# Paged decode attention interleaved with prompt attention, in bursts of decode steps behind whole head tiles

## The reference, cut to what matters

```python
def diff_attend(q, k, v, q_pos, k_pos, lam):
    s = jnp.einsum('bqhmd,bkhmd->bhmqk', q, k) * (DK_A ** -0.5)
    p = jax.nn.softmax(jnp.where(k_pos[None, :] <= q_pos[:, None], s, -jnp.inf), axis=-1)
    w = p[:, :, 0] - lam * p[:, :, 1]
    return jnp.einsum('bhqk,bkhd->bqhd', w, v)
# prompt: 8 query blocks of 128, 4 heads; sample: 4 new tokens, 4 heads,
pk = cache_k[page_table].reshape(DB, P, H_A, 2, DK_A)
pv = cache_v[page_table].reshape(DB, P, H_A, DV_A)
```

## Time and profile before

| | |
|---|---|
| median of 3 runs | 1150.35 us (1147.07 to 1150.73) |
| the profiled execution | 1145.49 us, span of the core 1143.9 us |
| granted TensorE clock over the span | 0.945 of full speed |
| PE busy | 1006.3 us, 88% of the span |
| DVE / ACT / POOL busy | 521.6 / 419.4 / 138.6 us |
| DMA | 142.08 MB, mean 124 GB/s |

### The profile page before, as it was taken

How to read it: one execution, slowest core, us unless ns; L and a number is a source line. 1 busy time by engine, 2 the same in 40 slices (tenths; PEclk the granted TensorE clock), 3 DMA queues, 4 the chain that set the end, 5 groups by cost and what they waited for, 6 DMA issues and landing times.

```text
span 1143.9 us, 19660 instructions
## 1 busy us (share of the span) xinstructions
PE 1006.3 (88%) x7424; PEld 801.5 (70%) x7424; DVE 521.6 (46%) x1212; ACT 419.4 (37%) x886; POOL 138.6 (12%) x290
## 2 busy tenths in 40 slices
PE   4779999999999999986887788577886999899997
PEld 3679989999888888864655555444555888577773
DVE  4523744554653445433433334167886533442222
ACT  4433353433245434342322223256665323321111
POOL 1300010000000000030333333301100000000000
PEclk8989999999999999988988988779999999999999
DMA  5351215111323222138998995492001032212210
GB/s 180 101 148 50 62 55 131 56 56 56 102 74 91 58 73 75 56 140 252 360 316 315 330 327 198 169 386 97 1 1 60 19 111 74 65 64 83 82 67 23
DMA packets 111249, 142.08 MB, mean 124 GB/s; under 512 B 9256, under 2 KB 75433, under 8 KB 111164
## 3 DMA queue, kind: packets, MB, share of 16 engines
q1 hardware_dynamic: 100924, 107.34, 29.2%
q0 software_dynamic: 10240, 33.56, 8.2%
HBM read 125.47 MB, written 15.41 MB: 123 GB/s over the span
## 4 chain that ended last, share of the span: by engine, by line
PE 69%; DVE 10%; DMA 8%; issue 6%; ACT 4%; POOL 2%; SPq 1%; POOLq 0%; ACTq 0%; DVEq 0%
PE ps L1600 59%; PE ps L1603 9%; DMA Vr<-in_cache_v 4%; DVE pp L1475 3%; DVE pp L1488 2%; DMA Kr<-in_cache_k 2%; DMA wst<-in_w_in 1%; DMA xrow<-in_x_prompt 1%; POOL si L648 1%; DVE hrow L1035 1%; DVE wlo L1041 1%; DVE st L1486 1%; PE ps L1595 1%; ACT on L947 1%; DMA out_k_prompt<-ktok 1%
## 5 line engine op out<-in xcount | busy, mean ns | idle before, releaser
L1600 PE MATMUL ps<-hhi,whi 128*128 128x272 f32 (+1 forms) x672 | 228.2, 340 | 7.0 <-DVE wlo L1041 5.9
L1600 PE MATMUL ps<-hhi,wlo 128*128 128x272 f32 (+1 forms) x672 | 219.0, 326 | 0.0
L1600 PE MATMUL ps<-hlo,whi 128*128 128x272 f32 (+1 forms) x672 | 218.3, 325 | 0.0
L1600 PE MATMUL ps<-wh,r 128*128 128x512 f32 (+1 forms) x576 | 163.3, 401 | 4.6 <-DVE wout_lo L1542 4.6
L1600 PEld LDWEIGHTS ps<-hhi,whi 128*128 128x128 f32 x672 | 128.9, 192 | 18.5 <-DVE wlo L1041 6.1
L1600 PEld LDWEIGHTS ps<-hlo,whi 128*128 128x128 f32 x672 | 128.9, 192 | 9.9 <-issue 1.9
L1600 PEld LDWEIGHTS ps<-hhi,wlo 128*128 128x128 f32 x672 | 128.5, 191 | 9.4
L1600 PEld LDWEIGHTS ps<-wh,r 128*128 128x128 f32 (+1 forms) x576 | 103.4, 182 | 34.4 <-issue 4.9
L1041 DVE TENSOR_TENSOR wlo<-wst,whi 128x1024 fp32r<-128x1024 f32 x56 | 68.6, 1225 | 88.0 <-ACT whi L679 88.0
L1401 DVE COPY kTs<-ps 128x512 f32<-128x512 f32 x64 | 44.3, 692 | 101.3 <-PE ps L1603 101.3
L617 POOL DMA_DIRECT2D Vr<-in_cache_v x128 | 69.1, 540 | 155.8 <-PE ps L1600 131.7
(11 more groups left out here) (307 smaller groups left out, 1542.7 us busy)
## 6 DMA issues: line engine op xcount, KB each, us to landing
Kr<-in_cache_k SPq DMA_DIRECT2D x128, 256.0 KB, 5.6
Vr<-in_cache_v POOLq DMA_DIRECT2D x128, 256.0 KB, 5.5
wst<-in_w_in SPq DMA_DIRECT2D x56, 512.0 KB, 3.9
out_y_prompt<-rows SPq DMA_DIRECT2D x16, 512.0 KB, 2.9
xrow<-in_x_prompt SPq DMA_DIRECT2D x8, 512.0 KB, 4.1
wout<-in_w_out SPq DMA_DIRECT2D x1, 4096.0 KB, 14.1
rows<-in_x_prompt SPq DMA_DIRECT2D x8, 512.0 KB, 4.3
wgate<-in_ple_gate_w SPq DMA_DIRECT2D x2, 2048.0 KB, 21.7
```

The costliest lines, as they stand in the source:

```text
L1600: return nc.tensor.matmul(out, lhsT, rhs, start=start, stop=stop)
```

## The change

The decode's stage is gone; its work is cut into 81 steps and put between the pieces of the prompt attention. Step n turns the keys of group n (over all sequences, 64 groups), turns a part of the weights of the sequence before (4 of its 17 turns in each of steps 3 to 6 of 8, the last in step 7), multiplies the values of group n-12, and scores group n-1. `SHARES` and `DECODED` say after which position steps are done: five lie among the 8 key-and-value pieces of the prompt, and 71 behind the last of the four phases of head tiles 0 to 31, in bursts of 1 (i = 0) to 3 or 4 (i = 7); the last five follow in the drain. Decode has banks 0 to 3 and the prompt attention 4 to 7: one pair of banks for keys (0, 1), one bank (2) for the scores, the turned weights and the `place_q` result, one (3) for values; one pair for head scores (4, 5), one bank (6) for turned weights, one (7) for values. `Kr` shrinks from 16 to 8 slots (4 groups), `S` is there twice (`S0`, `S1`). `w_out` is loaded after the last turn of decode weights, and the gate weights after the last head, since they take over those buffers. SP issues the prompt's key and value outputs and the key pages in the order of the positions.

```diff
+LAST_GROUP = NSEQ * GROUPS
+VALUES_LAG = 12
+STEPS_OF_DECODE = LAST_GROUP + VALUES_LAG + 5
+PHASES = 4
+SHARES = CH * [2.0] + [float(4 + u // H) if u < UNITS and phase == PHASES - 1 else 0.0 for u in range(UNITS + 4) for phase in range(PHASES)]
+POSITIONS = len(SHARES)
+DECODED = [min(STEPS_OF_DECODE - 5, round((STEPS_OF_DECODE - 5) * sum(SHARES[:pos + 1]) / sum(SHARES)))
+           + max(0, pos - POSITIONS + 6) for pos in range(POSITIONS)]
+DECODED = [min(n, STEPS_OF_DECODE) for n in DECODED]
+
+
+def stored(group):
+
+    return group + group // GROUPS + 1
+
+
+def comb_step(seq):
+
+    return GROUPS * (seq + 3) + 1 if seq < NSEQ - 1 else LAST_GROUP + VALUES_LAG + 1
+
+
+COMBINED = {comb_step(seq): seq for seq in range(NSEQ)}
...
+            def key_pages(n):
+                if n % 4 == 0:
+                    page[:] = nc.values_load_multi_w_load_instructions(
+                        ptab[0:1, n * GP:n * GP + GROUPS], engines=[mybir.EngineType.SP], min_val=0, max_val=POOL - 1)[1]
+                if n >= 4:
+                    sp.wait_ge(s["k_used"], n - 3)
+                for k in range(GP):
+                    sp.dma_start(Kr[:, GP * (n % 4) + k, :],
+                                 ck[bass.ds(page[GP * (n % 4) + k], 1), :, :].rearrange("o p d -> (o p) d")
+                                 ).then_inc(k_in[n % 4], 16)
...
+            for pos in range(POSITIONS):
+                if pos < CH:
+                    sp.wait_ge(s["kt_stored"], pos + 1)
+                    sp.dma_start(kp[pos * P:(pos + 1) * P, :], ktok[:, pos % 2, :]).then_inc(k_out[pos % 2], 16)
+                    sp.wait_ge(s["vt_stored"], pos + 1)
+                    put("out_v_prompt", vp[pos * P:(pos + 1) * P, :], vtok[:, pos, :])
+                for n in range(DECODED[pos - 1] if pos else 0, DECODED[pos]):
+                    if n + 4 < LAST_GROUP:
+                        key_pages(n + 4)
...
+            def attend(u, phase):
+                if phase == 0 and u >= 6 and u % H == 2:
+                    heads_square(u // H - 1)
+                if phase == 1 and u < UNITS and not two(u):
                     head_exp(u)
-                if 1 <= u <= UNITS:
-                    weights_out(u - 1)
-                if u >= 2 and (u - 2) % H == H - 1:
-                    heads_square((u - 2) // H)
+                if phase == 1 and 1 <= u <= UNITS:
+                    weights_out(u - 1, 0)
+                if phase == 2 and two(u - 1):
+                    weights_out(u - 1, 1)
+                if phase == 3 and two(u):
+                    head_exp(u)
+
+            for pos in range(POSITIONS):
+                if pos < CH:
+                    keys_out(pos)
+                else:
+                    attend(*divmod(pos - CH, PHASES))
+                for n in range(DECODED[pos - 1] if pos else 0, DECODED[pos]):
+                    decode(n)
...
+            def attend(u, phase):
+                if phase == 0 and u < UNITS:
+                    head_rows(u, 0)
+                if phase == 1:
+                    if u >= 6 and u % H == 2:
+                        heads_scale(u // H - 1)
+                    if u >= 7 and u % H == 3:
+                        heads_gate(u // H - 1)
+                    if 1 <= u <= UNITS:
+                        head_weights(u - 1)
+                if phase == 2 and two(u):
+                    head_rows(u, 1)
...
+            def keys(n):
+                pe.wait_ge(k_in[n % 4], 32 * (n // 4 + 1))
+                if n >= 1:
+                    pe.wait_ge(s["kT_act"], n)
+                    pe.wait_ge(s["kT_dve"], n)
+                for h in range(H):
+                    for k in range(GP):
+                        last = turn(ps[:, h // 2, ((h % 2) * GP + k) * P:((h % 2) * GP + k + 1) * P],
+                                    Kr[:, GP * (n % 4) + k, h * P:(h + 1) * P])
+                last.then_inc(s["k_used"], 1)
+            def scores(m):
+                i, g = divmod(m, GROUPS)
+                pe.wait_ge(s["kT_act"], m + 1)
+                pe.wait_ge(s["kT_dve"], m + 1)
+                if m:
+                    pe.wait_ge(s["s_stored"], stored(m) - 1)
+                else:
+                    pe.wait_ge(s["q8_ready"], NSEQ + 2 * H)
+                if i >= 1 and 2 <= g <= 6:
+                    pe.wait_ge(s["pT_act"], (i - 1) * 5 + g - 1)
+                if m + 1 in COMBINED:
+                    pe.wait_ge(s["as_added"], COMBINED[m + 1] + 1)
+                for h in range(H):
+                    last = mm(ps[32 * h:32 * h + 32, 2, 0:GP * PAGE], q8[:, i, h, :], kTs[:, m % 2, h, :])
+                last.then_inc(s["scores_ready"], 1)
...
+            def turn_weights(i, t):
+                if t == 0:
+                    pe.wait_ge(s["p_ready"], i + 1)
+                    if i >= 2:
+                        pe.wait_ge(s["as_added"], i - 1)
+                if (i + 1) * GROUPS + t + 1 < LAST_GROUP:
+                    pe.wait_ge(s["s_stored"], stored((i + 1) * GROUPS + t + 1))
+                else:
+                    pe.wait_ge(s["s_stored"], NSEQ * 9)
+                    if t:
+                        pe.wait_ge(s["pT_act"], i * 5 + t)
+                if t < 4:
+                    for k in range(4):
+                        last = turn(ps[:, 2, k * P:(k + 1) * P], S[i % 2][:, (4 * t + k) * P:(4 * t + k + 1) * P])
+                else:
+                    last = turn(ps[0:SMP, 2, 0:P], S[i % 2][:, PAST:PAST + SMP])
+                last.then_inc(s["pT_ready"], 1)
+            def combine(seq):
+                pe.wait_ge(s["ao_ready"], seq + 1)
+                pe.wait_ge(s["pT_act"], 5 * min(seq + 2, NSEQ))
+                pe.wait_ge(s["s_stored"], 9 * min(seq + 3, NSEQ))
+                mm(ps[:, 2, 256:256 + P].rearrange("p (h t) -> p h t", h=H), AO[:, :],
+                   place_q[:, :, 28 - seq * STEPS:28 - seq * STEPS + SMP]).then_inc(s["comb_ready"], 1)
+            def decode(n):
+                i, g = divmod(n, GROUPS)
+                if n < LAST_GROUP:
+                    keys(n)
+                if g >= 3 and 1 <= i <= NSEQ:
+                    turn_weights(i - 1, g - 3)
+                if 0 <= n - VALUES_LAG < LAST_GROUP:
+                    values(n - VALUES_LAG)
+                if n in COMBINED:
+                    combine(COMBINED[n])
+                if 1 <= n <= LAST_GROUP:
+                    scores(n - 1)
...
+
+            def head_scores(u, c):
                 i, h = divmod(u, H)
+                pair = PARTS_BEFORE[u] + c
+                first, k = part_of(u, c)
+                for m in range(2):
+                    if pair:
+                        pe.wait_ge(s["row_min"], 2 * pair - 1 + m)
+                    half = slice(64 * m, 64 * m + 64)
+                    mm(score_part(m, k), tok(QA + h, i * P, P, half), tok(KA + h, first, k, half)).then_inc(s["score_pair"], 1)
+
+            def head_turn(u, c):
+                first, k = part_of(u, c)
+                if c == 0:
+                    pe.wait_ge(s["w_done"], u + 1)
+                    if u >= 6 and u % H == 2:
+                        pe.wait_ge(s["a_done"], u // H)
+                if PARTS_BEFORE[u] + c:
+                    pe.wait_ge(s["wT_stored"], PARTS_BEFORE[u] + c)
+                for q in range(k // P):
+                    last = turn(ps[:, 6, q * P:(q + 1) * P], pp[:, u % 2, 0, first + q * P:first + (q + 1) * P])
+                last.then_inc(s["wT_ready"], 1)
+            def attend(u, phase):
+                if phase == 0:
+                    if u >= 7 and u % H == 3:
+                        heads_back(u // H - 1)
+                    if two(u):
+                        head_scores(u, 1)
+                    elif u + 1 < UNITS:
+                        head_scores(u + 1, 0)
+                if phase == 1 and 1 <= u <= UNITS:
+                    head_turn(u - 1, 0)
+                if phase == 2:
+                    if two(u - 1):
+                        head_turn(u - 1, 1)
+                    if two(u) and u + 1 < UNITS:
+                        head_scores(u + 1, 0)
+                if phase == 3 and 2 <= u < UNITS + 2:
                     head_values(u - 2)
+
+            for pos in range(POSITIONS):
+                if pos < CH:
+                    prompt_keys_and_values(pos)
+                else:
+                    if pos == CH:
+                        pe.wait_ge(s["kt_stored"], CH)
+                        pe.wait_ge(s["vt_stored"], CH)
+                        head_scores(0, 0)
+                    attend(*divmod(pos - CH, PHASES))
+                for n in range(DECODED[pos - 1] if pos else 0, DECODED[pos]):
+                    decode(n)
```

More of the change, by code:

```diff
@@ L892, in decode @@
-                if i < NSEQ:
-                    for g in range(2, GROUPS):
-                        keys(g)
-                if i >= 1:
-                    act.wait_ge(s["o_ready"], i)
-                    act.wait_ge(s["coef_ready"], i)
-                    if i >= 2:
```

(24 more changed lines are left out.)

564 lines of the change are left out of this document (222 added, 342 removed).

## The result

The changed kernel takes 1173.18 us in the median (1167.84 to 1173.8, 4 runs) where the kernel before takes 1150.01 (1147.07 to 1150.73): ratio 1.0196, interval 1.0161 to 1.0231. The forecast was 1138. The projection starts at 912.7 us instead of 884.5, and everything behind it is as long as before. So all of the loss, and 40 us against the forecast's 873, lies between 505 and 912 us.

What follows compares the result with a forecast made beforehand. Decode was taken to wait for pages, the head tiles for DVE. 30 + 137 - 1 + 20 + 156 + 19 + 7 = 368 us from 505 puts the projection at 873, about 12 us less: 1138 against the median, range 1120 to 1163.

Steps and rivals of the forecast that it cites:

- Clock: TensorE's clock drops after idle in root and short tiles, 2 us each; 7 us taken, between nothing and 15.
- Roots: Seven root tiles, where VectorE's scaling ahead of the weights waits for squares and root: 15.5 us, 20 with the gates.
- Slower by the clock: Rival, chance 0.20: waits inside every tile keep the clock at 0.85, costing 40 us, for 1171; at 0.92, 1154.
- the gates: Part of the root tiles' sum: the gates add 0.7 us seven times.
- Start: From 505 us to the first row minima at 535: 30 us, set by page and output transfers, covering TensorE's prompt pieces.
- End: From the last tile to the projection: weights, turns, values, root, `as_done` and the split of `w_out`, 19 us.
- Tiles and decode work: Head tiles with their joins to bursts, 137 - 1 us, and the decode steps done between them, 156 us.
- 7.0 + 2.4 a step: Sign for head-tile spacing in us by decode steps; differing by over 1 us would show the forecast wrong.

Runs made afterwards that it cites:

- e1: Changed kernel with GpSimd holding value pages until the root is issued and VectorE making the last tile's weights before scaling with the root; 1136.2 us.
- e7: Changed kernel with only GpSimd's value pages held until the root is issued, VectorE still scaling before the weights; 1155.4 us.
- e2: Changed kernel with extra unread matmuls on TensorE in tiles 17 to 31, ahead of the turns of the weights and of the second part; 1160.2 us.
- e5: e1 with extra unread matmuls in tiles 17 to 31, 5 ahead of the weights' turn and 3 ahead of the second part; 1135.4 us.
- e10: e1 with second-part turned weights in bank 0, and the first eight value pages issued only after the last prompt key copy; 1124.0 us.
- e12: e10 with decode steps in two places of a tile, and VectorE's weights moved ahead of the first phase's decode step; 1090.9 us.
- e3: Changed kernel with 76 of 81 decode steps in one row ahead of head tile 0, so the tiles run without steps between; 1197.6 us.

## Why the prediction was wrong, by its own steps

The sign was wrong. The terms that failed are **Clock** and **Roots**. No rival came as it was described. "Slower by the clock" is nearest, but it says 1154 us for a clock of 0.92 and 1171 for 0.85; from 541 to 884 us the clock was 0.91, for which its own working gives some 1156, and its sign, under 0.9 between 540 and 860 us, showed only from 670 to 752 (0.85). The other 17 us fit what roots, start and end took beyond their terms. (The prediction counts this case as the third in its list of signs, from the forecast on, and as the second under "Same", from the first rival on.)

- **Roots** (15.5 us and 4.9 for the gates). I took the chain from the end of before's head tiles, 2.54 us from the first square to the scaling, where GpSimd has an empty queue. In the changed kernel the value pages of each burst stand ahead of the root on GpSimd, at 0.57 us a page and 2.5 us where it reads new page numbers, and they wait there for TensorE to free their slots. The prediction has no term for that queue. Taking the root out of both queues removes 25.8 us of waits (e1). Of these 15.9 are VectorE's order, about what the term had (15.5), and 9.9, taken away first, are GpSimd's queue (e7), which it had at nothing.
- **Clock** (7 us). I counted a drop as 2 us and took 800 to 810 us of before as a sign that short pieces don't matter. After the wait at 869.67 half speed lasts the 8.3 us to 878, with TensorE busy for 7.55, so this drop costs about 3.8 us (an estimate, half of the busy time), not 2. The estimate from the rows gives 26 us at most where the term has 7. e2 takes 13 to 15 away while its own extra work still costs time; more was not shown. The Trainium skill, page "TensorE: Matmul & The Clock Gate", section "A second HAM failure mode: psum-queue depth-cycling", says that such micro-idles can make the clock oscillate. These runs agree in part. In e1, where from 606 to 840 us no wait for the weights is over 1.7 us, the clock is 0.92 from 670 to 840, and it is 1.00 and 0.98 when e5 fills the pieces. In the changed kernel itself the clock was also at half speed behind the long waits of the root tiles, which are no micro-idles.
- **Start** (first minima at 535). They came at 539.85. I had the megabytes right, but not who waits: the first prompt output, issued at 512.7 behind pages on all engines, is done at 526.8. Holding back eight value pages gives 4.5 us back (e10); a start with nothing changed in it varies by 3 to 4 us between runs.
- **End** (19 us). 22.5 from the last weights at 890.2 us. Two waits for value pages, 0.70 and 2.34 us, came while `w_out` was landing; I had put its cost at nothing. This cause was not tried by itself.
- **Tiles and decode work** (136 and 156 us). From e5's first minima (536.8) to its projection (872.4) are 336 us. Tiles, decode work, the gates' 4.9 and 23 for the end make 320, so 16 more are spent. Some 9 of them are clock, which is still 0.97 from 541 to 860 us (an estimate as above); waits of scores for row minima, 5.7 us in e5 and 6.1 in the changed kernel, and extra matmuls that run over are others. These were not told apart. The prediction's own sign for it showed: in block i = 6, with three steps a tile, the weights of the tiles come 14.3, 19.7 (the root tile), 17.9 and 16.0 us apart, where 7.0 + 2.4 a step gives 14.2. One slip in the sum is small: 0.1 us for each of 64 and 40 pieces is 10.4 us, where the prediction writes 8.
- **What held:** page waits fall from 30.4 to 3.0 us, the second part waits 0.75 us for ScalarE's copy, a full decode step takes 2.6 us where I had 2.4, the tail is unchanged.

The sum: start +5, roots +10 and end +4 are measured, which leaves 21 of the 40 us to clock, tiles and decode work. e2 shows 6 to 8 of them to be clock beyond the 7 that the forecast has, and the estimate from the rows allows up to 19. What lies between stays open. With the root out of the way the same merge is at 1136, near the forecast's 1138, but that is partly luck: there the root's wait is gone, for which the forecast has 15.5 us, and start, clock and end still cost more than it says. With four orders and one bank changed (e12) it is at 1091.

## What to carry to other kernels

When work is merged from two stages, write down for each small chain across engines (square, root, scale) what stands ahead of each link in its queue, page issues and register reads included, not just the duration of the link. On the engine that serves both, put first what the bound engine needs next: one call moved ahead of a copy was worth 29 us. And where the bound engine idles in pieces, compare the same matmul's duration before and after the gap: the slow work after a gap can cost half as much as the gap or more (about 3.8 us behind the wait of 7.04).

## What the runs showed of the hardware

- More work on TensorE made the kernel faster: with 3 to 14 useless matmuls in each of its gaps the granted clock of 670 to 752 us went from 0.85 to 1.00 and the time from 1173 to 1160 us (e2).
- The granted clock did not go with the work of the moment (e3). TensorE waited from 798.7 to 802.56 us, and the granted clock was 1.00 from 799 to 802. It worked from 802.56 on, and the clock was 0.50 from 803 to 808.5. From 809 to 812.5, with a wait of 1.66 us inside, it was 0.98, and from 813 to 818.9, with TensorE busy 98% of the time, 0.50 again.
- One kernel's time goes with its clock from run to run: e1's four runs took 1144.3, 1138.7, 1133.6 and 1133.2 us at granted clocks of 0.953, 0.958, 0.967 and 0.968.
- An output of 256 KB (`ktok`), issued at 512.7 us behind 8 key pages and beside 8 value pages, was done only at 526.8, and ScalarE waited 14.26 us for its buffer. With the value pages held back it waited 7.94 us (e10).
